# A gated recurrence's levels reordered: first level ahead of the context's states, the last two levels' blocks copied by ScalarE, the rest of a projection beside the output

## What is computed

```python
# per direction, head; f = lb + (1 - lb) * sigmoid(z), k = 1 - f, q = silu(.) / sqrt(128)
S_t = diag(f_t) S_{t-1} + k_t v_t^T          # S_0: the final state of the same scan over 256 context tokens
o_t = S_t^T q_t
mix_hg = rmsnorm(o_fwd + o_bwd) * norm_g * silu(g)
x = x + g1 * (concat(rmsnorm(hyena), mix_hg) @ w_out)
```

## Time and profile before

| | us |
|---|---|
| three runs | 2710.7, 2707.4, 2705.7 |
| median | 2707.4 |
| the profiled execution | 2705.3 |
| its span | 2703.5 |

### The profile page before, as it was taken

One profiled execution on the slowest core, in us unless ns is written; L12 is line 12 of the kernel. 1 busy time (PEld: TensorE's weight loads), 2 busy tenths in 40 slices (PEclk: granted clock), 3 DMA queues, 4 the chain that ended last, 5 costly groups with the idle time before them and its releaser, 6 DMA issues.

```text
span 2703.5 us, 34229 instructions
## 1 busy us (share of the span) xinstructions
PE 2337.0 (86%) x15038; PEld 1635.5 (60%) x15038; DVE 777.2 (29%) x1470; ACT 336.7 (12%) x601; POOL 8.7 (0%) x13
## 2 busy tenths in 40 slices
PE   7999889999999999999999999896667666666775
PEld 5888668888888789888886878651112222111121
DVE  5454544475000636521023238640000000000000
ACT  1101231012000222111001311110000000000000
POOL 0000000000000100000000000000000000000000
PEclk9999999999999999999999999978787877787778
DMA  8889234896445241034342223469999999999997
GB/s 354 359 342 378 114 141 177 360 358 258 152 155 187 93 140 35 4 140 175 136 168 83 78 64 127 184 271 427 427 428 428 426 428 427 427 428 427 428 428 337
DMA packets 70098, 709.51 MB, mean 262 GB/s; under 512 B 7776, under 2 KB 7904, under 8 KB 8672
## 3 DMA queue, kind: packets, MB, share of 16 engines
q1 hardware_dynamic: 69984, 707.79, 64.8%
HBM read 706.71 MB, written 1.05 MB: 262 GB/s over the span
## 4 chain that ended last, share of the span: by engine, by line
PE 63%; DMA 29%; DVE 7%; ACT 1%; issue 1%; SPq 0%; DVEq 0%
DMA arena<-in_experts 21%; PE ps L656 11%; PE ps L670 11%; PE ps L663 11%; PE ps L699 5%; DMA hT_sq<-in_experts 4%; PE ps L817 4%; PE ps L1013 4%; DMA ring<-in_experts 3%; PE ps L1225 2%; PE ps L1255 2%; PE ps L1189 1%; PE ps L629 1%; PE ps L1011 1%; DMA arena<-in_ada 1%; PE ps L715 1%
## 5 line engine op out<-in xcount | busy, mean ns | idle before, releaser
L1225 PE MATMUL ps<-arena 128*32 128x512 f32 x1376 | 220.8, 777 | 138.6 <-DMA arena<-in_experts 138.6
L656 PE MATMUL ps<-hT_sq,arena 128*128 128x256 f32 x1408 | 319.2, 380 | 4.2 <-ACT hT_sq L1332 4.2
L663 PE MATMUL ps<-hT_sq,arena 128*128 128x256 f32 x1408 | 318.3, 379 | 0.0
L670 PE MATMUL ps<-hid,arena 128*128 128x256 f32 x1408 | 311.1, 379 | 0.0
L656 PEld LDWEIGHTS ps<-hT_sq,arena 128*128 128x128 f32 x1408 | 266.7, 190 | 46.2 <-issue 10.4
L663 PEld LDWEIGHTS ps<-hT_sq,arena 128*128 128x128 f32 x1408 | 267.5, 190 | 36.4
L670 PEld LDWEIGHTS ps<-hid,arena 128*128 128x128 f32 x1408 | 267.5, 190 | 36.4
L1225 PEld LDWEIGHTS ps<-arena 128*32 128x32 f32 x1376 | 43.1, 127 | 311.0 <-DMA arena<-in_experts 221.9
L1678 DVE CUSTOM_DVE_ANT_0 hT_sq<-arena 128x1024 f32<-128x1024 f32 x184 | 213.4, 1220 | 11.5 <-DMA arena<-in_ada 11.0
L1304 ACT ACTIVATE arena<-ps 128x512 f32<-128x512 f32 (+5 forms) x146 | 87.3, 606 | 970.1 <-PE ps L1234 309.9
L1705 DVE TENSOR_TENSOR hid<-sil,ps 128x256 f32<-128x256 f32 x88 | 37.1, 421 | 566.8 <-ACT sil L1342 566.5
(11 more groups left out here) (358 smaller groups left out, 2172.3 us busy)
## 6 DMA issues: line engine op xcount, KB each, us to landing
arena<-in_experts SPq DMA_DIRECT2D x129, 2048.0 KB, 41.0
arena<-in_ada SPq DMA_DIRECT2D x96, 1024.0 KB, 10.3
ring<-in_experts SPq DMA_DIRECT2D x42, 2048.0 KB, 40.9
ring<-in_ring_w SPq DMA_DIRECT2D x52, 1024.0 KB, 5.0
arena<-in_ffn_gate SPq DMA_DIRECT2D x44, 1024.0 KB, 6.1
arena<-in_ffn_up SPq DMA_DIRECT2D x44, 1024.0 KB, 6.3
arena<-in_ffn_down SPq DMA_DIRECT2D x44, 1024.0 KB, 4.8
hT_sq<-in_experts SPq DMA_DIRECT2D x21, 2048.0 KB, 40.5
```

The costliest lines, as they stand in the source:

```text
L656: last = mm(ps[:, ft, 0:T], gate3[:, kt, ft * P:(ft + 1) * P], h3[:, kt, :], start=kt == 0, stop=kt == KT - 1)
L663: last = mm(ps[:, ft, T:2 * T], up3[:, kt, ft * P:(ft + 1) * P], h3[:, kt, :], start=kt == 0, stop=kt == KT - 1)
L670: last = mm(acc(m), down3[:, ft, m * P:(m + 1) * P], hid3[:, ft, :], start=False, stop=True, skip_group_check=True)
L1225: last = mm(ps[32 * n:32 * n + 32, part, :], e_xe[:, kt, :], w[:, (kt % 2) * SLOT + n * 512:(kt % 2) * SLOT + (n + 1) * 512], start=kt == ...
```

## The change

`hyena_back` moves ahead of the last unit of `b2_in` on both engines. In `hgrn` the first level comes first, then the context's transposes (now into banks 0 to 3); the states are computed behind the first round's matmuls, and the pieces `beside` start with the second round, so that pieces 12 and 13 fall behind the cross blocks and 14 and 15 behind the sums of squares, where `keep_clock` was. VectorE copies F at once; in level 0 K is g_k itself, and E is set by a fill and a copy from F behind a wait for the transposes. From round 6 on ScalarE copies the blocks of a level (only those that count: four pieces of 32 partitions for each direction, then two of 64) and signals `hg_copied`; VectorE waits for `hg_level` there. In round 7 E is not updated, and the product q * F goes to `g_E` in the same round. The output's matmuls with `g_X` come last for each pair of heads. A Sqrt of one element stands behind the first Square on ScalarE. VectorE scales the first two heads' sums, and the others' behind the first head. `x_kt` and `x_v` get other room.

```diff
@@ -422,8 +422,8 @@
         x_f, x_k, x_E = g_F, g_E, g_Q
-        x_kt = ar(B1 + 12288, 2048).rearrange("p (d t c) -> p d t c", d=2, t=TT)
-        x_v = tiles(ar(B1 + 15360, 1024), HYW)
+        x_kt = ar(B1 + 17408, 2048).rearrange("p (d t c) -> p d t c", d=2, t=TT)
+        x_v = tiles(ar(B1 + 1024, 1024), HYW)
@@ -515,6 +515,7 @@
         B2_GATED = max(u for u, unit in enumerate(B2_UNITS) if unit[1] in ("zf", "zb", "q")) + 1
+        MASKED = 6
@@ -992,6 +993,8 @@
                         hyena_turn()
+                    if u == B2_FIRST - 1:
+                        hyena_back()
@@ -1031,6 +1034,7 @@
                         pe.wait_ge(sem("b2_evac"), len(B2_UNITS))
+                        pe.wait_ge(sem("hg_state_s"), 2)
@@ -1041,69 +1045,77 @@
-                pe.wait_ge(sem("hg_gates"), 1)
-                pe.wait_ge(sem("b2_evac"), B2_FIRST)
-                pe.wait_ge(sem("hy_mixed"), 4)
-                for d in range(2):
+                def level(d, kk, qq):
...
                         for h in range(HGH):
-                            last = tr(ps[:, 4 + 2 * d + tt, h * P:(h + 1) * P], x_k[:, d, h, tt * P:(tt + 1) * P], ident)
-                        last.then_inc(sem("hg_ctx_t"), 1)
-                beside(0)
-                pe.wait_ge(sem("hg_ctx_kt"), 4)
-                for d in range(2):
+                            last = mm(ps[:, 4 + 2 * d + tt, h * P:(h + 1) * P],
+                                      kk[:, d, h, tt * P:(tt + 1) * P], qq(d)[:, h, tt * P:(tt + 1) * P],
+                                      start=True, stop=True)
+                    last.then_inc(sem("hg_level"), 1)
+                def state(d):
+                    if d == 0:
+                        pe.wait_ge(sem("hg_ctx_kt"), 4)
...
                     last.then_inc(sem("hg_state"), 1)
-                beside(1)
-                def level(d, kk, qq):
+                pe.wait_ge(sem("hg_gates"), 2)
+                pe.wait_ge(sem("hy_mixed"), 4)
+                for d in range(2):
+                    level(d, g_k, lambda d: g_q)
+                pe.wait_ge(sem("b2_evac"), B2_FIRST)
+                for d in range(2):
...
                         for h in range(HGH):
-                            last = mm(ps[:, 4 + 2 * d + tt, h * P:(h + 1) * P],
-                                      kk(d)[:, h, tt * P:(tt + 1) * P], qq(d)[:, h, tt * P:(tt + 1) * P],
-                                      start=True, stop=True)
-                    last.then_inc(sem("hg_level"), 1)
-                pe.wait_ge(sem("hg_gates"), 2)
-                for d in range(2):
-                    level(d, lambda d: g_k[:, d], lambda d: g_q)
-                pe.wait_ge(sem("hg_state_s"), 2)
+                            last = tr(ps[:, 2 - 2 * d + tt, h * P:(h + 1) * P], x_k[:, d, h, tt * P:(tt + 1) * P], ident)
+                        last.then_inc(sem("hg_ctx_t"), 1)
...
-                        pe.wait_ge(sem("hg_taken"), 2 * lev + d + 1)
+                        if lev < MASKED:
+                            pe.wait_ge(sem("hg_taken"), 2 * lev + d + 1)
+                        else:
+                            pe.wait_ge(sem("hg_copied"), 2 * (lev - MASKED) + d + 1)
                         pe.wait_ge(sem("hg_scaled"), 2 * lev + d + 1)
-                        level(d, lambda d: g_K[:, d], lambda d: g_Q[:, d])
-                        beside(2 + 2 * lev + d)
+                        level(d, g_K if lev else g_k, lambda d: g_Q[:, d])
+                        if lev == 0:
+                            state(d)
+                        else:
+                            beside(2 * lev - 2 + d)
+                pe.wait_ge(sem("hg_copied"), 2 * (NLEV - MASKED) + 1)
...
                                   g_Q[:, d, h, (1 - d) * P:(2 - d) * P], start=True, stop=True)
-                last.then_inc(sem("hg_cross"), 1)
-                pe.wait_ge(sem("hg_cross_s"), 1)
-                pe.wait_ge(sem("hg_taken"), 2 * NLEV + 2)
+                    if d == 1:
+                        last.then_inc(sem("hg_cross"), 1)
+                    beside(2 * NLEV - 2 + d)
+                pe.wait_ge(sem("hg_copied"), 2 * (NLEV - MASKED) + 2)
                 pe.wait_ge(sem("hg_scaled"), 2 * NLEV + 3)
-                for h in range(HGH):
-                    o, e0 = half(6, h), slice(h * P, (h + 1) * P)
-                    mm(o, g_S[0][:, h, :], g_Q[:, 0, h, :], start=h % 2 == 0, stop=False, skip_group_check=True)
-                    mm(o, g_S[1][:, h, :], g_Q[:, 1, h, :], start=False, stop=False, skip_group_check=True)
-                    for d in range(2):
-                        for tt in range(TT):
-                            mm(o[:, tt * P:(tt + 1) * P], g_v[:, tt, e0], g_A[:, d, tt, h, :],
-                               start=False, stop=False, skip_group_check=True)
-                        last = mm(o[:, (1 - d) * P:(2 - d) * P], g_v[:, d, e0], g_X[:, d, h, :],
-                                  start=False, stop=d == 1, skip_group_check=True)
-                    if h % 2:
-                        last.then_inc(sem("hg_out"), 1)
+                for b in range(2):
+                    for h in (2 * b, 2 * b + 1):
+                        o, e0 = half(6, h), slice(h * P, (h + 1) * P)
+                        mm(o, g_S[0][:, h, :], g_E[:, 0, h, :], start=h % 2 == 0, stop=False, skip_group_check=True)
+                        mm(o, g_S[1][:, h, :], g_E[:, 1, h, :], start=False, stop=False, skip_group_check=True)
+                        for d in range(2):
+                            for tt in range(TT):
+                                mm(o[:, tt * P:(tt + 1) * P], g_v[:, tt, e0], g_A[:, d, tt, h, :],
+                                   start=False, stop=False, skip_group_check=True)
+                    pe.wait_ge(sem("hg_cross_s"), 1)
+                    for h in (2 * b, 2 * b + 1):
+                        for d in range(2):
+                            last = mm(half(6, h)[:, (1 - d) * P:(2 - d) * P], g_v[:, d, h * P:(h + 1) * P], g_X[:, d, h, :],
+                                      start=False, stop=d == 1, skip_group_check=True)
+                    last.then_inc(sem("hg_out"), 1)
...
                     mm(ps[:, 4 + b, :], ones, sq[:, b * 512:(b + 1) * 512], start=True, stop=True).then_inc(sem("hg_out"), 1)
-                keep_clock(6, 8)
+                    beside(14 + b)
@@ -1288,7 +1300,6 @@
             b2_in()
-            hyena_back()
@@ -1488,7 +1501,7 @@
                     act.wait_ge(sem("hg_ctx_t"), i + 1)
-                    copy(x_kt[:, i // 2, i % 2, :], ps[:, 4 + i, :]).then_inc(sem("hg_ctx_kt"), 1)
+                    copy(x_kt[:, i // 2, i % 2, :], ps[:, (i + 2) % 4, :]).then_inc(sem("hg_ctx_kt"), 1)
@@ -1497,6 +1510,16 @@
                         .then_inc(sem("b2_evac"), 1)
+                for lev in range(MASKED, NLEV + 1):
+                    hb = 1 << lev - 1
+                    for d in range(2):
+                        act.wait_ge(sem("hg_level"), 2 * lev + d + 1)
+                        for tt in range(TT):
+                            src = ps[:, 4 + 2 * d + tt, :].rearrange("p (h s) -> p h s", s=P)
+                            for lo in range(0, P, 2 * hb):
+                                early, late = (slice(lo + hb * i, lo + hb * (i + 1)) for i in ((0, 1) if d == 0 else (1, 0)))
+                                last = copy(g_A[early, d, tt, :, late], src[early, :, late])
+                        last.then_inc(sem("hg_copied"), 1)
@@ -1504,6 +1527,8 @@
                     f(sq3[:, 2 * b:2 * b + 2, :], g_F[:, 0, 2 * b:2 * b + 2, :], ACT.Square).then_inc(sem("hg_os"), 1)
+                    if b == 0:
+                        f(small[:, 224:225], ones[:, 0:1], ACT.Sqrt)
@@ -2004,11 +2028,7 @@
-                dve.wait_ge(sem("hg_ctx_t"), 4)
-                cp(g_F, g_f)
-                done(nc.vector.memset(g_E, 1.0))
-                dve.wait_ge(sem("hg_state"), 2)
+                done(cp(g_F, g_f))
@@ -2032,25 +2052,40 @@
                         late, early = sides(d)
-                        taken(lev, d)
-                        tt_(cut(g_Q[:, d], late), cut(g_q, late), cut(g_F[:, d], late), ALU.mult)
-                        tt_(cut(g_K[:, d], early), cut(g_k[:, d], early), cut(g_E[:, d], early), ALU.mult).then_inc(sem("hg_scaled"), 1)
+                        if lev < MASKED:
+                            taken(lev, d)
+                        else:
+                            dve.wait_ge(sem("hg_level"), 2 * lev + d + 1)
+                        last = tt_(cut(g_Q[:, d], late), cut(g_q, late), cut(g_F[:, d], late), ALU.mult)
+                        if lev > 0:
+                            last = tt_(cut(g_K[:, d], early), cut(g_k[:, d], early), cut(g_E[:, d], early), ALU.mult)
+                        last.then_inc(sem("hg_scaled"), 1)
...
                         edge_e = cut(g_F[:, d], early)[:, :, end:end + 1].to_broadcast([P, HGH * T // (2 * hb), hb])
+                        if lev == 0:
```

(21 more changed lines are left out.)

## The result

| | before | after |
|---|---|---|
| median of five runs, us | 2708.2 (2705.7 to 2710.7) | 2693.1 (2690.8 to 2696.6) |
| span of the profiled execution | 2703.5 | 2694.8 |

The ratio is 0.9945 (95% interval 0.993 to 0.9959), 15 us. A second set of five runs on another occasion gave a median of 2691.9, against 2707.4 for the kernel before, and a ratio of 0.9939 (0.9926 to 0.9953). The forecast was 2690.0 (2684 to 2697), the gain in it 17.4.

The account below looks back on a forecast made before the run. The experts' transfer stream, moving with its first slot, bounds the end; VectorE narrowly bounds the stage ahead. Gains 10.3 - 1.1 + 4.4 + 2.9 + 0.9 = 17.4 us gave 2687.9, plus 2.1 for the median: 2690.0 (2684 to 2697).

Parts of the forecast that it names:

- The stream moves 1 to 1 with its first slot: Experts' transfers: an earlier first expert moves the whole stream and the end equally; slots under 18 us late cost nothing.
- Start, 10.3: Stage start: the first level follows the last input unit directly, VectorE's first take at 1637.55 instead of 1647.86, gaining 10.3 us.
- Level 0: First level's processing on VectorE: 1.75 us lost waiting for transposes, fill and copy 1.0 together; gain shrinks to 9.2 us.
- TensorE takes VectorE's place: Levels 6 and 7: VectorE's half-levels shrink, so TensorE bounds with a chain of 16.04 us; gain grows to 13.6.
- Masked copies are free: Levels 6 and 7: ScalarE's copies take at most 1.6 us per half, free below 3.5.
- Output at full clock, 8.8: Output matmuls: four heads take 8.8 us instead of 11.7, the waits being filled; gain grows to 16.5.
- Tail 5.15, TensorE last: Last output matmul to projection: TensorE needs 5.15 us, the first head 4.7, against 6.13 before; gain grows to 17.4.
- The clock did follow in the output: Rival for the output: the clock falls there even so, costing 3 to 7 us, 2695 us; chance 0.12.
- it didn't stay up in the routing: Rival for the routing: the clock stays up there, at most 9 us less, 2681 to 2688; chance 0.05.
- no slot or masked copy held anything up: Two rivals: a slot over 18 us late, 2703 to 2708, chance 0.04; slow masked copies, 2695 to 2699, chance 0.05.

Follow-up runs that it names:

- no_copy: The changed kernel with VectorE taking the blocks of levels 6 and 7 as it does the others, instead of ScalarE's masked copies; 2695.0 us.
- ctx_first: The changed kernel with the context's 16 transposes ahead of the first level instead of behind it; 2692.3 us.
- end_clock: The changed kernel with 12 matmuls on zeros ahead of each wait for the last expert's last three slots; 2690.4 us.
- tail_old: The changed kernel with VectorE scaling all four sums first and the Sqrt table loaded at the first root; 2692.7 us.

## Why the prediction was right, and where it was off

- **The stream moves 1 to 1 with its first slot.** Right: 905.4 us within 0.2 in fourteen profiles, though the projection slots' last wait put the first two expert slots at 1685.02. That is 1681.4 on the axis of before, as late as foreseen.
- **Start, 10.3.** Right: VectorE's first take is 10.35 us earlier.
- **Level 0.** The wait of 1.75 was 1.71. The fill and copy were costed at 1.0 together, bounds 0.75 and 1.4; they took 0.80 (1644.73 to 1645.53). This term was mis-sized. The 0.80 is nearer to the quarter of the 2048-element rows than to the middle I took, and the estimate of 1.1 from the Trainium skill ("VectorE: DVE Perf Modes", The TRN2 errata) was further off. The profile before had what sizes the fill: its fills took 0.272 us for 256 elements (L1804, without a stride) and 1.765 for 2048 (L2009), which on a straight line is 0.485 for 512, and 0.485 is what each of the two took. The gain at level 1 is 9.7 (1649.73 is 39.16 behind the first "i" unit, 1655.82 was 48.87) instead of 9.2. Of these 0.5 us fill and copy give 0.45; 0.17 is a slip of adding, as the prediction's own terms lead to 1646.48 and not 1646.65; and other rows take 0.1 back.
- **TensorE takes VectorE's place.** Right, by the chain of 15.85 us (16.04 forecast), and by no_copy: 3.2 instead of 5.0.
- **Masked copies are free.** Right: 1.10 and 0.65 us a half, and TensorE never waits for them.
- **Output at full clock, 8.8.** Right for after (1704.24 to 1713.06). Off for before: the 11.7 I set against it held in one execution only. In the two others the output took 10.9, and the cross blocks ahead of it 0.7 less. This is the other term that was mis-sized: the stage is worth 18.2 against the first profile, 16.7 to 16.8 against the others. The prediction treated a slow stretch of the clock as a fixed cost of the waits, when its place against the work is not the same in each execution. Too much here and too little in level 0 and the chain: that the forecast 17.4 lies between 16.8 and 18.2 is in part luck.
- **Tail 5.15, TensorE last.** Right: measured 5.17 (1713.06 to 1718.23), VectorE ready 4.8 behind. Without the tail's change it is 7.10.
- **Rivals.** The clock did follow in the output; it didn't stay up in the routing, and no slot or masked copy held anything up.
- **How much of the stage is shown by undoing it.** Undone one at a time, the copies, the hyena rows, the level's place and the tail give 3.2, 1.6, 1.0 and 1.9, together 7.7 of the 16.8 to 18.2. Another 7.1 rests on the difference and the rows told with ctx_first. What remains, 2.0 to 3.4, is by size the output at full clock and, against the first profile, the slow cross block. That the filled waits keep the clock up there is not shown: no run takes out the pieces alone, and in no_copy the output stayed at full clock behind a wait of 1.45 us.
- **From 17.4 forecast to 15 in the median.** Outside S, the six profiles of the changed kernel and its variants without zeros have 2578.7 to 2587.1 us (mean 2582.2) and the three of before 2577.7 to 2582.6 (mean 2580.9). With S at 124.9 on average before, the stage is worth 17.2, and less these 1.3 that is 16 us; by the medians the two sets gave 15.1 and 15.5. The 1.3 is within the scatter of nine profiles, so nothing is shown there.

## What to carry to other kernels

When the end of a kernel is one saturated stream of transfers, look for its first free slot, and shorten the latency stage ahead of it; the gain can be checked by a single distance between two instructions. In the changed kernel it repeats to 0.04 us, where medians of five runs can't tell 2; in the kernel before, with half clock inside it, it moved by 1.4. When work is taken off the engine that bounds a loop, add up the next engine's chain before counting the gain: 5.0 us off VectorE were worth 3.2. A stretch at half clock in one profile is no constant: take it from several before it enters a sum.

## What the runs showed of the hardware that was not expected

The start of the stage differs by up to 3.9 us between executions (1606.7 to 1610.6) and the end by 4.3 (12.4 to 16.7), in unchanged code. At the end 3.4 us of it are the same matmuls at one or the other clock, and 0.9 lies behind the last of them. The granted clock fell to 0.50 in the routing in all fourteen profiles. In the ten without zeros there it fell 0.2 to 2.6 us behind the end of a wait of 1.83 us, and the later, the shorter was the stretch from the output projection to the first slot given back: 0.2 us and 55.1 in end_clock, 0.9 and 54.4 in after, 2.6 and 52.8 in tail_old. So this column's scatter is the clock's moment as well. In the four with that wait filled it fell all the same, with TensorE busy for 2.83 us or more of the window 1744 to 1747 and for all of the next, and in two of them with full-size matmuls between the routing's own. A fill of fp32 on VectorE took 0.272, 0.485 and 1.765 us for 256, 512 (with a stride of two) and 2048 elements: about 0.06 us and 0.83 ns an element. And a load of the Sqrt table cost 1.28 us with the next instruction 0.02 behind it, while the Square that followed (1713.88) needed no other.
